# Recurrent jobs of a hybrid trunk step: the inverse's transpose turned by TensorE and copied by ScalarE at each level, in place of a product and an addition

## The chip, the cores and the metric

The kernel runs on one core of one Trainium2 chip. The metric is the device time of one execution in microseconds; the time before is the median of three runs, 2041.28 us (2039.77 to 2044.31).

## The reference, cut to what matters

The program is one inference step of a two-layer trunk over 640 tokens (512 latent, 128 context), all in float32. Layer 0 is attention, layer 1 is a recurrent mixer (a WKV scan and an SSD scan side by side), and each layer ends in a convolutional feed-forward block. The change lies in the WKV scan, which runs once forward and once backward for each of 8 heads of width 64:

```python
def step(S, inp):
    r_t, w_t, a_t, b_t, k_t, v_t = inp
    sa = jnp.einsum('bhvk,bhk->bhv', S, a_t)
    S = S * w_t[:, :, None, :] + sa[..., None] * b_t[:, :, None, :] + v_t[..., None] * k_t[:, :, None, :]
    return S, jnp.einsum('bhvk,bhk->bhv', S, r_t)
```

The kernel does this in chunks of 64 tokens. Within a chunk the coupling of the tokens through `sa` is a triangular 64x64 system, and its inverse is needed for each head, direction and chunk.

## The kernel before, in words

TensorE, VectorE, ScalarE and GpSimd each run a program written out by hand; they meet only at semaphores. The WKV scan is eight jobs (n = 0 to 7): a pair of heads (j = n // 2, one head on partitions 0 to 63, the other on 64 to 127) in one direction (d = n % 2). A job holds ten chunks in two groups g of five. Its tiles are `G_` (the gram products, the first 64 columns of which are the triangular matrix), `X_` (the inverse so far), `XT_` (its transpose), `V_` and the PSUM banks `VX(g)` and `TT(g)`.

The inverse is built in five levels, doubling the block size at each. Per level and group, in the order of `wkv_order`:

- "v": TensorE multiplies `G_` by `X_` into `VX` (ten products of 64x64x64, five chunks by two heads), and VectorE multiplies that by the level's mask into `V_` (line 2587, here "the mask").
- "xt", first half, at levels 1 to 4: TensorE multiplies `XT_` and `V_` into `VX`, and VectorE adds the result to `X_` (line 2593).
- "xt", second half, at all levels: TensorE multiplies `V_` and `XT_` into `TT`, and VectorE adds the result to `XT_` (line 2596).

`wkv_order` is one list of pieces, and all engines walk it in that order. It gives a job 20 slots: for each level "v" of group 0, "v" of group 1, "xt" of group 0, "xt" of group 1. The table `BESIDE` puts pieces of the next job (+1) and of the job before (-1) behind each slot, so that TensorE has other products to do while VectorE masks and adds. Those that matter here are:

- behind slot 3: "scan" of the next job (VectorE line 2538, a scan over 650 elements that waits for GpSimd's line 2657; ScalarE lines 2453 and 2454, two exponentials that wait for the scan);
- behind slots 6 to 8: "prod" of the next job (VectorE lines 2550 to 2569); the last piece also has a copy on ScalarE (line 2460) that waits for the last of these;
- behind slots 7, 9 and 11, when the next job is even: "vt", three turns of values on TensorE, each evacuated by ScalarE (lines 2471 and 2472);
- behind slot 10: "atok" of the next job (TensorE line 2301, which waits for the last "prod"; ScalarE line 2478);
- behind slot 11: "gram" of the next job (TensorE; two of the three banks 4 to 6, which rotate over all side pieces).

Job 0 also carries pieces that run once (`ONCE`), and job 7 has no next job beside it. The names "job n" and "slot" below are these.

Weights of the low-rank factors of the recurrent mixer (`w2s`, `a2s`, `g2s`) are loaded by GpSimd's queue, lines 2955 to 2958, behind five loads of constants and states; TensorE's `first_lora` waits for the semaphore `lora_loaded`, VectorE's `decay_dve` for `ssd_loaded`.

## Time and profile before

| | |
|---|---|
| median of 3 runs | 2041.28 us |
| lowest, highest | 2039.77, 2044.31 us |
| the profiled execution's own time | 2041.86 us |
| its span | 2039.9 us |
| its mean granted TensorE clock | 0.984 |
| TensorE, VectorE, ScalarE, GpSimd busy | 96%, 55%, 34%, 7% of the span |

The profile is of one execution. Its span runs from the first to the last recorded instruction; the execution's own time is 2 us longer. A float32 product appears in the trace as two weight loads (PEld) and two matmuls (PE) when it is an ordinary product, so ten products are 20 records. A matmul's record includes its way through the array, so a row of PE is busier than the array; the weight loads start when the work starts. "Idle before" in the brackets names what ended the wait.

### The profile page before, as it was taken

Reading aid. Unit: us, or ns where it says so; the run is one execution under the profiler, and the core shown is the slowest. Engines: PE = TensorE matmul, PEld = TensorE weight load, DVE = VectorE, ACT = ScalarE, POOL = GpSimd, SP = SyncE. Lnnn points to the kernel's source line nnn. Section 1 sums busy time; section 2 is a strip of 40 time slices with the busy share of each in tenths; the row PEclk is TensorE's granted clock in tenths of the full one; section 3 lists DMA queues with packets and bytes.
Section 4 is the critical chain, followed back from the end, with each engine's and each line's share of the span. In section 5 each row is a group of like instructions: output and inputs, shape, how many; then the busy total and the mean of one; then the engine's idle time right before and its main releaser. Section 6 shows DMA issues by size and latency. Waiting matters only on the chain.

```text
span 2039.9 us, 41373 instructions
## 1 busy us (share of the span) xinstructions
PE 1965.0 (96%) x18397; PEld 1745.2 (86%) x18397; DVE 1115.6 (55%) x2046; ACT 688.9 (34%) x1239; POOL 137.4 (7%) x130
## 2 busy tenths in 40 slices
PE   5999999999999999999999799999999999999997
PEld 3695444899999999999997688888858999999997
DVE  3226754475545562354555877777646555556223
ACT  2322554353323341232346523333204333334111
POOL 2000000000000000000004512222000000000000
PEclk7999999999999999999999899999999999999999
DMA  9123738312222222332220000000211221122322
GB/s 338 49 83 133 271 107 301 109 49 76 83 83 83 68 60 58 85 100 64 62 73 24 7 3 3 3 4 3 91 33 51 83 83 62 63 83 58 86 58 79
DMA packets 141921, 163.92 MB, mean 80 GB/s; under 512 B 2496, under 2 KB 107120, under 8 KB 141744
## 3 DMA queue, kind: packets, MB, share of 16 engines
q1 hardware_dynamic: 138592, 149.96, 22.8%
q0 software_dynamic: 3152, 11.32, 1.5%
q8 instruction: 145, 2.38, 0.5%
q14 instruction: 32, 0.26, 0.0%
HBM read 157.52 MB, written 3.75 MB: 79 GB/s over the span
## 4 chain that ended last, share of the span: by engine, by line
PE 87%; DVE 9%; DMA 1%; issue 1%; ACT 1%; POOL 0%; DVEq 0%; SPq 0%; ACTq 0%; POOLq 0%
PE ps L226 83%; DMA ring<-in_ada_w 1%; DVE g_lo L865 1%; DVE work L2538 1%; PE ps L1253 1%; DVE small L1388 1%; DVE work L498 1%; PE ps L347 1%; ACT work L1317 0%; DVE work L2064 0%; PE ps L462 0%; PE ps L2283 0%; PE ps L2301 0%; DVE work L2596 0%; DVE w_lo L729 0%
## 5 line engine op out<-in xcount | busy, mean ns | idle before, releaser
L226 PE MATMUL ps<-x_hi_r,w_lo 128*128 128x320 f32 (+3 forms) x2240 | 521.8, 308 | 1.6 <-DVE x_lo_r L504 1.3
L226 PE MATMUL ps<-x_hi_r,w_hi 128*128 128x320 f32 (+2 forms) x1792 | 428.8, 311 | 0.9 <-issue 0.9
L226 PE MATMUL ps<-x_lo_r,w_hi 128*128 128x320 f32 (+2 forms) x1792 | 424.9, 308 | 0.0
L226 PEld LDWEIGHTS ps<-x_hi_r,w_lo 128*128 128x128 f32 (+1 forms) x2240 | 373.8, 187 | 3.9 <-DVE x_lo_r L504 1.9
L226 PE MATMUL ps<-work 64*64 64x64 f32 (+6 forms) x4602 | 314.3, 259 | 15.1 <-ACT work L1317 6.7
L226 PEld LDWEIGHTS ps<-x_lo_r,w_hi 128*128 128x128 f32 x1792 | 305.6, 188 | 0.0
L226 PEld LDWEIGHTS ps<-x_hi_r,w_hi 128*128 128x128 f32 x1792 | 303.8, 188 | 1.4 <-issue 1.3
L226 PEld LDWEIGHTS ps<-work 64*64 64x64 f32 (+4 forms) x4602 | 210.7, 145 | 101.1 <-issue 60.0
L678 DVE SCALAR_TENSOR_TENSOR work<-ps,par,work 128x511 f32<-128x511 f32 (+1 forms) x188 | 103.3, 550 | 255.7 <-ACT work L829 245.8
L729 DVE TENSOR_TENSOR w_lo<-ring,w_hi 128x1024 fp32r<-128x1024 f32 (+1 forms) x152 | 158.6, 1079 | 89.3 <-ACT w_hi L718 89.2
L718 ACT ACTIVATE w_hi<-ring 128x1024 fp32r<-128x1024 f32 (+1 forms) x152 | 135.6, 937 | 207.5 <-DMA ring<-in_ffn_down 185.4
L829 ACT ACTIVATE work<-ps,par 128x640 f32<-128x640 f32 x88 | 77.9, 885 | 376.1 <-PE ps L226 376.1
L226 PE MATMUL ps<-g_lo,w_hi 128*128 128x320 f32 (+2 forms) x704 | 174.7, 309 | 0.0
L226 PE MATMUL ps<-work,ring 64*64 64x64 f32 (+3 forms) x2368 | 119.2, 235 | 5.5 <-ACT work L384 2.9
L226 PEld LDWEIGHTS ps<-g_lo,w_hi 128*128 128x128 f32 x704 | 121.4, 188 | 0.0
L226 PEld LDWEIGHTS ps<-work,ring 64*64 64x64 f32 (+2 forms) x2368 | 93.2, 140 | 29.2 <-issue 23.5
L448 DVE SCALAR_TENSOR_TENSOR h<-ps,mods,h 128x512 f32<-128x512 f32 (+2 forms) x76 | 34.9, 495 | 140.0 <-PE ps L226 139.9
L226 PE MATMUL ps<-x_lo_r,w_lo 128*128 128x320 f32 (+2 forms) x416 | 108.2, 310 | 0.0
L680 DVE SCALAR_TENSOR_TENSOR work<-ps,par,work 128x511 f32<-128x511 f32 (+1 forms) x188 | 103.4, 550 | 6.7
L226 PE MATMUL ps<-x_hi_r,w_in_hi 128*128 128x320 f32 (+1 forms) x384 | 89.5, 315 | 0.4 <-issue 0.4
L226 PE MATMUL ps<-x_lo_r,w_in_hi 128*128 128x320 f32 (+1 forms) x384 | 88.0, 310 | 0.0
L226 PE MATMUL ps<-ring,cond 128*32 128x512 f32 x384 | 56.7, 675 | 18.6 <-DMA ring<-in_ada_w 18.6
(378 smaller groups left out, 2452.9 us busy)
## 6 DMA issues: line engine op xcount, KB each, us to landing
ring<-in_ada_w SPq DMA_DIRECT2D x24, 2048.0 KB, 8.0
ring<-in_ffn_up SPq DMA_DIRECT2D x44, 1024.0 KB, 7.0
ring<-in_ffn_down SPq DMA_DIRECT2D x16, 1408.0 KB, 7.0
ring<-in_l_w_in SPq DMA_DIRECT2D x11, 1024.0 KB, 5.2
ring<-in_l_w_out SPq DMA_DIRECT2D x4, 2048.0 KB, 7.9
ring<-in_l_w_in SPq DMA_DIRECT2D x3, 2048.0 KB, 9.0
h<-in_xT POOLq DMA_DIRECT2D x1, 2560.0 KB, 14.7
out_yT<-work POOLq DMA_DIRECT2D x2, 768.0 KB, 4.0
```

The costliest lines, as they stand in the source:

```text
L226: return pe.matmul(out, lhsT, rhs, start=first, stop=last)
L347: ins = pe.matmul(ps_all[:, 1024 * pair + heads * c:1024 * pair + heads * c + heads], squares[:, P * c:P * c + P], col, start=first and c ...
L448: ins = dve.scalar_tensor_tensor(h(m, x, y), psum(u % 2, x, y), gate(m, c), h(m, x, y), ALU.mult, ALU.add)
L498: ins = dve.scalar_tensor_tensor(hn(t, x, y), h(t, x, y), gain(t, c), bank(6 + p)[:, x - a:y - a], ALU.mult, ALU.mult)
L678: ch(dve.scalar_tensor_tensor(acc(a + 1, b), psrc(a, b - 1), w0, acc(a + 1, b), ALU.mult, ALU.add))
L680: ins = dve.scalar_tensor_tensor(acc(a, b - 1), psrc(a + 1, b), w2, acc(a, b - 1), ALU.mult, ALU.add)
L718: act.activation(wh_b[:, SLOT * (f % 2) + w * part:SLOT * (f % 2) + w * part + w], ring[:, SLOT * (n % RING) + w * part:SLOT * (n % RING) ...
L729: dve.tensor_tensor(wl_b[:, at:at + w], ring[:, at:at + w], wh_b[:, SLOT * (f % 2) + w * part:SLOT * (f % 2) + w * part + w].bitcast(F32), ...
L829: act.activation(tile(cacc, 2 * (m % 2) + half), spair(n % 3, cut=up_cut(n)), ACT.Identity, bias=pc(f"ffn_b{l}", half * FT + m), scale=cw( ...
L865: dve.tensor_tensor(gl(t), G(t), gh(t).bitcast(F32), ALU.subtract).then_inc(sg("g_lo"), 1)
L1253: ins = pe.transpose(bank(4)[:, P * kt:P * kt + P] if kt < 4 else bank(5, P), pb[:, P * kt:P * kt + P], ident[:, :])
L1388: dve.tensor_reduce(small[:, c:c + 1], pair_ap(i % 2, 0, w), AXX, ALU.max, negate=True)\
```

## The change

At levels 2 to 5, the transpose is no longer kept up by its own product and addition. TensorE multiplies `X_` (as the stationary operand) by the identity into `TT` at the head of "v", and ScalarE copies `TT` into `XT_` (a new branch of its program at the same place in the list). The "xt" pieces of levels 1 to 4 lose their second product, and VectorE loses its additions of line 2596 there. Level 5 keeps the product and the addition, since the result needed there is the transpose after the last level. The semaphore `wkv_tu` counts two a job instead of ten, and a new one, `wkv_tc`, counts the copies; "xt" of levels 2 to 5 waits for it. Beside that, the three loads of low-rank weights count on `ssd_loaded`, and `first_lora`, `decay_dve` and GpSimd wait for all eight loads.

```diff
@@ TensorE, wkv_pe, kind == "v"
+                    if lev > 1:
+                        for c in range(5 * g, 5 * g + 5):
+                            for e in range(2):
+                                p0, p1 = ROWS[e]
+                                ins = mm(pe, TT(g)[p0:p1, c - 5 * g, :], X_(n)[p0:p1, c, :], ident[p0:p1, p0:p1])
+                        ins.then_inc(sg("wkv_t"), 1)
...
@@ TensorE, wkv_pe, kind == "xt"
-                    if lev > 1 or n > 0:
-                        pe.wait_ge(sg("wkv_tu"), 10 * n + 2 * (lev - 2) + g + 1)
+                    if lev > 1:
+                        pe.wait_ge(sg("wkv_tc"), 8 * n + 2 * (lev - 2) + g + 1)
+                    elif n > 0:
+                        pe.wait_ge(sg("wkv_tu"), 2 * (n - 1) + g + 1)
...
-                    for c in range(5 * g, 5 * g + 5):
-                        for e in range(2):
-                            p0, p1 = ROWS[e]
-                            ins = mm(pe, TT(g)[p0:p1, c - 5 * g, :], V_[p0:p1, c, :], XT_(n)[p0:p1, c, :])
-                    ins.then_inc(sg("wkv_t"), 1)
+                    else:
+                        for c in range(5 * g, 5 * g + 5):
+                            for e in range(2):
+                                p0, p1 = ROWS[e]
+                                ins = mm(pe, TT(g)[p0:p1, c - 5 * g, :], V_[p0:p1, c, :], XT_(n)[p0:p1, c, :])
+                        ins.then_inc(sg("wkv_t"), 1)
@@ ScalarE, wkv_act
+                elif kind == "v" and i[0] > 1:
+                    lev, g = i
+                    act.wait_ge(sg("wkv_t"), 10 * n + 2 * (lev - 2) + g + 1)
+                    act.activation(XT_(n)[:, 5 * g:5 * g + 5, :], TT(g), ACT.Copy).then_inc(sg("wkv_tc"), 1)
@@ VectorE, wkv_dve, kind == "xt"
-                    dve.wait_ge(sg("wkv_t"), 10 * n + 2 * (lev - 1) + g + 1)
-                    x = XT_(n)[:, 5 * g:5 * g + 5, :]
-                    dve.tensor_tensor(x, x, TT(g), ALU.add).then_inc(sg("wkv_tu"), 1)
+                    else:
+                        dve.wait_ge(sg("wkv_t"), 10 * n + 8 + g + 1)
+                        x = XT_(n)[:, 5 * g:5 * g + 5, :]
+                        dve.tensor_tensor(x, x, TT(g), ALU.add).then_inc(sg("wkv_tu"), 1)
@@ VectorE, decay_dve
-            dve.wait_ge(sg("ssd_loaded"), 16 * 5)
+            dve.wait_ge(sg("ssd_loaded"), 16 * 8)
@@ TensorE, first_lora
-                pe.wait_ge(sg("lora_loaded"), 48)
+                pe.wait_ge(sg("ssd_loaded"), 16 * 8)
```

On ScalarE, in job 2 between the exponentials of "scan" and the copies of "atok" (line 2460 is the copy at the end of "prod", line 2478 evacuates "atok"), before:

```order
L2453 ACTIVATE stat<-work 128x650 [waits wkv_scan]
L2454 ACTIVATE work<-work 128x650
L2460 ACTIVATE work<-work 64x10x64 [waits wkv_prod]
L2478 ACTIVATE work<-ps 64x5x64 [waits wkv_atok]
L2478 ACTIVATE work<-ps 64x5x64
```

And of the change, where the same copy of "prod" is line 2469, "atok" is line 2487 and the new copy is line 2495:

```order
L2462 ACTIVATE stat<-work 128x650 [waits wkv_scan]
L2463 ACTIVATE work<-work 128x650
L2495 ACTIVATE work<-ps 128x320 [waits wkv_t] x3
L2469 ACTIVATE work<-work 64x10x64 [waits wkv_prod]
L2495 ACTIVATE work<-ps 128x320 [waits wkv_t]
L2487 ACTIVATE work<-ps 64x5x64 [waits wkv_atok]
```

Three of the new copies (level 2, both groups, and level 3, group 0) stand behind the exponentials, and the fourth (level 3, group 1) behind the copy of "prod".

On TensorE, in job 2 from "prod" to the first "gram" of the next job (`work,ring` are the products of "v", `work 64x64` those of "xt" and of the chain, 128x64 is "atok", `work 128x128 x8` is "gram"), before:

```order
L226 MATMUL ps<-work,ring 64x64 x20
L226 MATMUL ps<-work 64x64 x22
L2301 MATMUL ps<-ident,work 128x64 x10
L226 MATMUL ps<-work 64x64 x20
L226 MATMUL ps<-work 128x128 x8
L226 MATMUL ps<-work 64x64 x2
L226 MATMUL ps<-work,ring 64x64 x10
```

And of the change:

```order
L226 MATMUL ps<-work 64x64 x12
L2301 MATMUL ps<-ident,work 128x64 x10
L226 MATMUL ps<-work 64x64 x10
L226 MATMUL ps<-work 128x128 x8
L226 MATMUL ps<-work 64x64 x2
L226 MATMUL ps<-ident,work 64x64 x10
L226 MATMUL ps<-work,ring 64x64 x10
```

Ten products go from each "xt" piece, and ten with the identity come at the head of each "v" piece of levels 2 to 5: the count over a job stays the same.

## Rows read from the trace of the kernel before

**Rows 1.** The page's first part: busy us, share of the span, instructions.
```profile
PE 1965.0 (96%) x18397; PEld 1745.2 (86%) x18397; DVE 1115.6 (55%) x2046; ACT 688.9 (34%) x1239; POOL 137.4 (7%) x130
```

**Rows 2.** Busy time by window, one window for each job: jobs 0, 2, 3; sum of eight.
```profile
core 0: us, PE busy (x) PEld busy (x) DVE busy (x) ACT busy (x) POOL busy (x), PEclk, DMA share, GB/s
1161.70:1201.00 39.30, 33.68 (x760) 29.73 (x760) 29.66 (x62) 11.83 (x22) 11.29 (x9) 0.91 0.01 3
...
1239.40:1277.00 37.60, 36.15 (x958) 32.89 (x959) 28.57 (x65) 11.74 (x28) 10.60 (x9) 1.00 0.02 4
1277.00:1315.10 38.10, 37.75 (x969) 34.10 (x969) 28.46 (x64) 13.70 (x34) 8.62 (x7) 1.00 0.01 3
...
sum 291.50, PE 280.32 PEld 254.79 DVE 220.03 ACT 90.92 POOL 68.97; mean PE 35.04 PEld 31.85 DVE 27.50 ACT 11.36 POOL 8.62
```

**Rows 3.** By source line: ns min/median/max of the addition and of a ScalarE copy.
```profile
L2596 DVE TENSOR_TENSOR work<-work,ps x80: 475/489/492, 1166.6 to 1453.3; 128x320 f32<-128x320 f32 x80
L2486 ACT ACTIVATE work<-ps x16: 438/438/439, 1160.1 to 1426.9; 128x320 f32<-128x320 f32 x16
```

**Rows 4.** Timeline, job 2: products with the identity (start us, us, what).
```profile
1273.24 0.67 PEld L226 LDWEIGHTS ps<-ident,work 64*64 64x64 f32 x20
```

**Rows 5.** DMA issues (KB each, us to landing) from 896 us; VectorE's first use.
```profile
work<-in_l_g POOLq DMA_DIRECT2D x1, 256.0 KB, 4.3
...
L1795 DVE TENSOR_SCALAR work<-work x1: 485/485/485, 1009.0 to 1009.0; 104x640 f32<-104x640 f32 x1
```

**Rows 6.** Timeline, job 2, from level 1's "xt" to the scan.
```profile
1243.20 2.75 PEld L226 LDWEIGHTS ps<-work 64*64 64x64 f32 x88 [0.44 <-DVE work L2587]
...
1244.00 1.01 POOL L2657 TENSOR_SCALAR work<-work 128x320 f32<-128x320 f32 x1 [2.21 <-ACT work L2447]
...
1246.20 2.78 DVE L2538 TENSOR_TENSOR_SCAN work<-work 128x650 f32<-128x650 f32 x1
```

**Rows 7.** Timeline, job 2, level 3, up to "gram".
```profile
1256.50 0.66 PEld L226 LDWEIGHTS ps<-work,ring 64*64 64x64 f32 x20 [0.36 <-DVE work L2593]
...
1258.03 0.37 PEld L226 LDWEIGHTS ps<-work 64*64 64x64 f32 x10 [0.76 <-DVE work L2587]
...
1259.57 0.16 DVE L2569 COPY work<-stat 128x2 f32<-128x2 f32 x1
...
1259.64 0.48 DVE L2587 TENSOR_TENSOR work<-ps,work 128x320 f32<-128x320 f32 x1
1259.77 0.73 ACT L2460 ACTIVATE work<-work 64x640 f32<-64x640 f32 x1 [9.37 <-DVE work L2569]
1259.78 0.39 PEld L2301 LDWEIGHTS ps<-ident,work 64*128 64x128 f32 x10 [0.51 <-DVE work L2569]
...
1260.24 1.61 PEld L226 LDWEIGHTS ps<-work 64*64 64x64 f32 x44
...
1261.55 0.97 PEld L226 LDWEIGHTS ps<-work 64*128 64x128 f32 x16
```

**Rows 8.** Timeline, job 3, level 3, up to "gram".
```profile
1297.22 0.74 ACT L2460 ACTIVATE work<-work 64x640 f32<-64x640 f32 x1 [2.53 <-DVE work L2565]
...
1297.70 1.24 PEld L226 LDWEIGHTS ps<-work 64*64 64x64 f32 x40
...
1298.65 0.88 ACT L2478 ACTIVATE work<-ps 64x320 f32<-64x320 f32 x2
...
1299.65 0.52 PEld L226 LDWEIGHTS ps<-work 64*128 64x128 f32 x7 [0.33 <-issue]
```

**Rows 9.** Timeline, job 0, levels 2 to 3.
```profile
1170.07 1.38 PE L226 MATMUL ps<-work 64*64 64x64 f32 x40 [1.23 <-DVE work L2587]
...
1170.32 0.73 ACT L2454 ACTIVATE work<-work 128x650 f32<-128x650 f32 x1
...
1176.31 0.80 PE L226 MATMUL ps<-work,ring 64*64 64x64 f32 x20 [1.96 <-DVE work L2593]
...
1179.94 2.40 PE L226 MATMUL ps<-work 64*64 64x64 f32 x40
```

**Rows 10.** Busy time by window in job 0 (columns as in rows 2).
```profile
1172.00:1178.00 6.00, 3.14 (x82) 2.63 (x80) 5.96 (x13) 0.00 (x0) 1.43 (x2) 0.96 0.00 0
1178.00:1184.00 6.00, 5.21 (x71) 4.61 (x73) 5.89 (x15) 1.43 (x3) 0.00 (x0) 0.50 0.02 4
```

More of the change, by code:

```diff
@@ L2357, in wkv_pe @@
                         ins.then_inc(sg("wkv_x"), 1)
-                    for c in range(5 * g, 5 * g + 5):
-                        for e in range(2):
-                            p0, p1 = ROWS[e]
-                            ins = mm(pe, TT(g)[p0:p1, c - 5 * g, :], V_[p0:p1, c, :], XT_(n)[p0:p1, c, :])
-                    ins.then_inc(sg("wkv_t"), 1)
+                    else:
[4 more added lines that the diff above has]
+                        ins.then_inc(sg("wkv_t"), 1)
                 elif kind == "uw":
                     c0, c1 = THIRD[i]
-                    pe.wait_ge(sg("wkv_tu"), 10 * n + (9 if c1 <= 5 else 10))
+                    pe.wait_ge(sg("wkv_tu"), 2 * n + (1 if c1 <= 5 else 2))
                     pe.wait_ge(*evacuated("lkv", n, 1))
@@ L2957, in _ @@
                              (g2s, t_in["l1_g2"])):
-                pool.dma_start(dst, src).then_inc(sg("lora_loaded"), 16)
-            pool.wait_ge(sg("lora_loaded"), 48)
+                pool.dma_start(dst, src).then_inc(sg("ssd_loaded"), 16)
+            pool.wait_ge(sg("ssd_loaded"), 16 * 8)
             first_sum_pool(pool, Chain(pool, "pool_chain"))
```

## The prediction

> **What bounds the kernel now.** I read the page first: TensorE is busy 96% of the span, VectorE 55%, ScalarE 34% [rows 1]. That average says nothing of the stage that changes, so the next view is busy time by window, one window a job [rows 2]. The eight jobs fill 291.5 us, and TensorE is busy for 280.3 of them: 11.2 us are left in which it does nothing. Of those, job 0 has 5.6 (39.30 - 33.68), an even job like job 2 1.45, an odd job like job 3 0.35, and job 7 none. VectorE is busy 28 of 38 us in a job, ScalarE 12 to 14. So TensorE sets the pace, and VectorE makes it wait only in places. The timeline shows where: in job 2 at the second "v" of level 3 (0.36 us for line 2593), at its first "xt" (0.76 us for the mask), at "atok" (0.51 us for the last "prod") [rows 7]. These three make up most of the job's 1.45, and all lie in the stretch from the scan to "atok", in which VectorE has the next job's scan and products in its queue. From "gram" on TensorE hardly waits.
>
> **TensorE's work does not shrink.** Per level and group ten products with the identity replace ten others, 64 sets out and 64 in (8 jobs, 4 levels, 2 groups). Twenty weight loads with the identity take 0.67 us [rows 4], of which the last one's tail is about 0.1, so 0.58 a set. Eighty-eight loads of the "xt" kind take 2.75 us [rows 6]: 0.6 for twenty. Difference: 0. A cheap turn is on view too, ten records for ten turns: "atok", 0.39 us [rows 7]. If the new turns cost that, the sum would fall by 64 x 0.28 = 18 us; the code issues ordinary products, so I take 0. The Trainium skill (TensorEngine Tiling (Array Packing), Restrictions) states that column tiling disables the transpose mode for fp32 input; these outputs fill 64-partition tiles, so by it the -18 us isn't there to be had, and by row and rule alike the sum stays where it is.
>
> **VectorE loses 64 additions** of 0.49 us [rows 3], 0.40 when others follow closely: 26 us. They are worth only what TensorE waited for VectorE, at most the 11.2 us. **ScalarE gains 64 copies**; its copies of this shape take 0.44 us [rows 3], 28 us on an engine that is free two thirds of the stage. But each is now between the turn and "xt", in a queue that is served in order. Two places in the list matter. The level 2 copies stand behind the two exponentials, which wait for the scan; the copy of level 3, group 1 stands behind the copy of "prod" (0.73 us), which waits for the last "prod". I therefore walk three kinds of job.
>
> **Even job (2, 4, 6).** Level 1's "xt" starts at 1243.20 [rows 6]. Without the second products, X of group 1 ends at 1244.4, its addition at about 1245.0, and the scan can start when GpSimd's 1244.00 + 1.01 is done: 1245.1, not 1246.20, so 1.1 earlier. Behind the scan VectorE has two fewer additions before the last "prod", but has to wait a little for TensorE's products; I carry 1.3. The last "prod" (ended 1259.7) ends at 1258.4, and "atok" starts there. Then ScalarE: copy of "prod" 1258.45 to 1259.2, new copy to 1259.65, and only then "xt" of group 1, at 1259.7 (before: 1260.24, after its mask at 1259.64 + 0.48 [rows 7]). Ten products and "gram" follow at about 1260.5, against 1261.55. That is 1.05 earlier, but at this point the old kernel has done six sets for the transpose and the new one four, so 2 x 0.58 = 1.16 are still owed. Net +0.1 a job, three jobs: **+0.3**. What VectorE gave back, the wait for ScalarE takes.
>
> **Odd job (1, 3, 5).** VectorE was hardly late here, so it can give back only the waits at level 2. The copy of "prod" (1297.22 [rows 8]) moves to about 1295.9 and ends at 1296.6; the new copy ends at 1297.05, about when "xt" of group 1 could start. The evacuations of "vt" (0.8) and "atok" (0.88 [rows 8]) stand behind it and end at 1298.7. "Gram" needs the banks of "atok": 1298.75, not the 1298.4 that TensorE would reach. Before: 1299.65. 0.9 earlier less 1.16 owed: +0.26, three jobs: **+0.8**.
>
> **Job 0.** The second exponential ends at 1171.05 and the new copy at 1171.5; "xt" of level 2, at 1170.07 before, waits for it: 1.4 later. VectorE's chain behind it (6 us, which ended in the wait of 1.96 at 1176.31 [rows 9]) starts 0.7 later, saves 0.4 and 0.4 in two additions, and at "gram" I find 0.8 earlier less 1.16 owed: **+0.4**.
>
> **Job 7** has no side work of a next job: a wait for the mask goes (the turn now covers it) and one for the addition to `X_` comes, both some 0.1 to 0.2 us: 0. From level 4 on the copies have a turn, a "v" and side pieces as cover (over 1.5 us for a 0.44 us copy): 0; with less cover each would cost up to 0.44.
>
> **The loads.** They are issued from 897 us, and the last takes 4.3 us to land; VectorE first needs them at 1009.0 [rows 5], TensorE later: 0.
>
> **Sum:** 0.3 + 0.8 + 0.4 + 0 = +1.5 us on the profiled execution's 2041.86, which is 0.6 above the median. On the median: 2041.28 + 1.5 = **2042.8 us**. Its uncertainty is that of a walk, 0.3 to 0.4 a job. A measurement here tells about 0.2%, 4.1 us, from no change.
>
> **Rivals.**
> - *ScalarE's queue decides (slower).* The walks rest on VectorE getting 1.3 us earlier. Each 0.1 us less moves "xt" of group 1, and "gram" with it, 0.1 later in every job with a next one, since the two copies then end the wait. If only the scan's own wait is saved in part (0.6, one set on TensorE), "xt" of group 1 starts at 1259.77 - 0.6 + 0.73 + 0.44 = 1260.35, 0.65 later than in the walk: 7 x 0.7 = 4.9 us on top of 1.5, **2047.7 us**. With nothing gained it would be 7 x 1.3 = 9.1 on top, 2051.9. It decides from 1.3 us downward. For it: both copies surely stand there, and the products that VectorE waits for come from TensorE. Against: the scan waits for two additions of line 2596 ahead of it, which go. Chance 0.13.
> - *VectorE's relief reaches TensorE (faster).* If ScalarE's copies hide, the waits on VectorE go: at most -11.2 [rows 2], 2030; half of that is likelier, as turns and "vt" pieces also wait for other things: **2035.7 us**. Against: the two places in ScalarE's queue. Chance 0.08.
> - *The clock falls (slower).* In job 0 it stands at half from 1178 to 1184, after a stretch in which TensorE was busy 3.14 of 6 us [rows 10]; forty matmuls then take 2.40 us, not 1.38 [rows 9]. If the new turns were to leave the stage at the lower level, each job would be longer by tens of us, over 2200 in all; if only job 0's stretch grows by half, +1.5. Against the first: the identity products of rows 4 ran in a job at clock 1.00 [rows 2]. The Trainium skill (TensorE: Matmul & The Clock Gate, Part 4: PE-mode transpose) says that transpose-mode work doesn't count as busy for the clock; by it a fifth of the inverse's products would cease to count, though these are ordinary products. Chance 0.02 for the large case.
> - *The edit doesn't relieve anything (same).* That is in my walk; it needs no time of its own.
>
> **How the numbers follow.** The forecast has 0.77, with its own range 2038.5 to 2047; it leaves 0.02 below 2037.2 and 0.07 above 2045.4. Faster: 0.07 of the second rival and 0.01 to 0.02 of the forecast's tail: 0.08. Slower: 0.13 + 0.02 + 0.07 = 0.22. Same: 0.70. Range for 8 in 10: 2038.5 to 2048.5, which takes in the queue's rival and leaves out the faster one and the clock.
>
> **What would show it.** Right: 16 rows of line 2596's successor instead of 80, and 64 new ScalarE copies of 0.44 us; TensorE's busy time in the jobs unchanged within 1 us; the scan about 1.1 us earlier in its job; the idle before level 3's "xt" of group 1 ended by ScalarE, some 0.7 us, in the even jobs; job periods within 0.5 us of 37.65 and 38.1. Wrong: "xt" of group 1 released by VectorE and periods under 37.2 (second rival), or periods of 38.3 and more (first), or a clock under 1.00 past job 0. If a set of turns takes over 0.65 us, the term of TensorE's work is wrong, by 64 times the excess.

## The result, and the profile after

| | before | changed |
|---|---|---|
| median of 16 runs each, us | 2040.92 | 2044.93 |
| lowest to highest, us | 2039.24 to 2044.31 | 2038.47 to 2051.42 |
| profiled execution, us (span) | 2041.86 (2039.9) | 2051.21 (2049.4) |
| mean granted clock over the span | 0.984 | 0.984 |

The changed kernel is slower by a ratio of 1.0021, 95% interval 1.0012 to 1.0029: some 4 us, which is right at the 0.2% that a measurement here can tell from no change. The forecast was +1.5 us and a range of 2038.5 to 2048.5 us: the time lies in the range and near the bound between the cases "same" and "slower", but the forecast has less than half of the loss. The mean clock of the span, which has the rest of the program in it, doesn't show the difference. Note also the spread: the standard deviation is 3.0 us over these 16 runs, against 1.7 here and 2.3 to 2.5 in series of 28 to 35 runs of the kernel before. The profiled execution is one of the slowest, so it holds more of the loss than the median does, and I read it beside the profile of a second measurement of the same kernel (e10 below: 2045.38 us). Below, one execution of e9 and one of e12 took several milliseconds; both are left out, and the figures of these two runs rest on eleven.

The first part of the page, busy time by engine, answers to [rows 1]:

```profile
PE 1970.3 (96%) x18397; PEld 1751.2 (85%) x18397; DVE 1084.0 (53%) x1982; ACT 715.0 (35%) x1303; POOL 143.5 (7%) x130
```

TensorE has the same number of instructions, VectorE has 64 fewer, ScalarE 64 more, as foreseen. Busy time by window, one window a job (jobs 0 to 3, 6 and 7, and the sum of eight), answers to [rows 2]:

```profile
core 0: us, PE busy (x) PEld busy (x) DVE busy (x) ACT busy (x) POOL busy (x), PEclk, DMA share, GB/s
1163.80:1206.60 42.80, 35.77 (x760) 31.39 (x762) 26.75 (x55) 14.96 (x30) 11.29 (x9) 0.88 0.01 2
1206.60:1244.70 38.10, 37.36 (x969) 33.91 (x969) 24.82 (x57) 16.98 (x42) 9.89 (x7) 1.00 0.02 3
1244.70:1284.10 39.40, 37.42 (x958) 34.20 (x960) 24.88 (x58) 15.02 (x36) 11.78 (x9) 0.96 0.01 3
1284.10:1322.20 38.10, 37.36 (x969) 33.91 (x969) 24.31 (x56) 16.97 (x42) 9.88 (x7) 1.00 0.01 3
...
1399.80:1437.60 37.80, 35.83 (x960) 32.81 (x962) 24.79 (x57) 15.02 (x36) 11.81 (x9) 1.00 0.01 3
1437.60:1461.20 23.60, 23.51 (x694) 22.59 (x692) 13.65 (x36) 6.26 (x17) 0.00 (x0) 1.00 0.02 5
sum 297.40, PE 282.13 PEld 257.06 DVE 188.38 ACT 117.21 POOL 76.31; mean PE 35.27 PEld 32.13 DVE 23.55 ACT 14.65 POOL 9.54
```

The eight windows take 297.4 us; those of [rows 2] took 291.5, but the last of them ran 1.6 us past job 7's last mask, so the table below, with the same ends for both, is the one to compare: 289.9 and 297.4. The reader is to see three things. VectorE is busy 32 us less over the span (1084.0 against 1115.6) and nothing comes of it. Jobs 1, 3 and 6 are within 0.5 us of the walk. And jobs 0 and 2 (job 4 reads like job 2) stand out, both with a granted clock below 1.00: 0.88 where [rows 2] had 0.91, and 0.96 where they had 1.00.

For a finer table I took each job from its first mask of level 1 to that of the next job; job 7 from its first mask to its last. All from profiled executions, us:

| job | 0 | 1 | 2 | 3 | 4 | 5 | 6 | 7 | sum |
|---|---|---|---|---|---|---|---|---|---|
| before | 39.31 | 38.33 | 37.65 | 38.11 | 37.65 | 38.11 | 37.65 | 23.10 | 289.9 |
| changed | 42.75 | 38.16 | **39.35** | 38.17 | **39.38** | 38.16 | 37.84 | 23.54 | 297.4 |
| changed, e10 | 39.23 | 38.16 | **39.31** | 38.16 | **39.38** | 38.17 | 37.84 | 23.54 | 293.8 |

Jobs 2 and 4 carry a stretch of half clock in both profiles of the changed kernel; job 6, which has the same program, doesn't, and takes 37.84. So an even job has two parts: +0.19 that the program costs, and +1.5 that the clock costs. Job 0 varies most, and of all things it is the one that differs between the two profiles. One caution on reading a whole execution from its profile: the program ahead of job 0 is the same in all kernels here but for the wait for the loads, and yet the first mask of job 0 starts anywhere from 1155.1 to 1165.2 us over the fourteen profiles. Of the 9.5 us between the spans of the two profiles above, 2.1 lie ahead of job 0.

**An even job without a clock fall.** The timeline of job 6, level 3, answers to [rows 7]:

```profile
1418.86 0.16 DVE L2582 COPY work<-stat 128x2 f32<-128x2 f32 x1
...
1418.93 0.48 DVE L2600 TENSOR_TENSOR work<-ps,work 128x320 f32<-128x320 f32 x1
1419.05 0.73 ACT L2469 ACTIVATE work<-work 64x640 f32<-64x640 f32 x1 [3.51 <-DVE work L2582]
1419.07 0.39 PEld L2301 LDWEIGHTS ps<-ident,work 64*128 64x128 f32 x10 [1.09 <-DVE work L2582]
...
1419.81 0.44 ACT L2495 ACTIVATE work<-ps 128x320 f32<-128x320 f32 x1
...
1420.36 2.04 PEld L226 LDWEIGHTS ps<-work 64*64 64x64 f32 x40 [0.91 <-DVE work L2600]
1420.39 2.15 PE L226 MATMUL ps<-work 64*64 64x64 f32 x40 [0.80 <-ACT work L2495]
```

It went as the walk said: the last "prod" ends at 1419.02, ScalarE copies it, then makes the new copy until 1420.25, and only then does TensorE go on with "xt" of group 1, 0.80 us of idle that its own row puts down to line 2495. (The weight loads' row names VectorE's mask, which had ended at 1419.41; the copy came last.) What the walk had too kindly: "prod" comes 1.13 us earlier in its job (1419.02 - 1399.78 against 1259.73 - 1239.36), not 1.3, and "xt" 0.30 earlier, not 0.54. Ahead of "atok" TensorE idles 1.09 us where it idled 0.51 [rows 7], since it has 0.58 us less to do before it.

**An odd job.** Timeline of job 3, which answers to [rows 8]:

```profile
1303.58 0.44 ACT L2495 ACTIVATE work<-ps 128x320 f32<-128x320 f32 x1
...
1304.16 0.80 PE L226 MATMUL ps<-work 64*64 64x64 f32 x20 [0.44 <-ACT work L2495]
...
1304.71 0.88 ACT L2487 ACTIVATE work<-ps 64x320 f32<-64x320 f32 x2
...
1305.70 1.32 PEld L226 LDWEIGHTS ps<-work 64*128 64x128 f32 x20 [0.51 <-issue]
```

"Gram" starts 21.63 us into the job (1305.70 - 1284.07) where it started at 22.64 (1299.65 - 1277.01): 1.01 earlier, against 0.9 in the walk, less the 1.16 still owed. The job is 0.06 longer.

**Job 0.** Timeline at level 2, which answers to [rows 9]:

```profile
1171.62 0.47 DVE L2600 TENSOR_TENSOR work<-ps,work 128x320 f32<-128x320 f32 x1
...
1172.39 0.73 ACT L2463 ACTIVATE work<-work 128x650 f32<-128x650 f32 x1
...
1173.03 0.74 ACT L2495 ACTIVATE work<-ps 128x320 f32<-128x320 f32 x2
...
1173.59 1.33 PE L226 MATMUL ps<-work 64*64 64x64 f32 x20 [2.46 <-ACT work L2495]
```

Here too the wait is the one foreseen: the mask ends at 1172.09, the copy behind the second exponential at about 1173.5, and "xt" goes 1.5 us later than the mask would let it. Behind it the clock comes in. Job 0 of e10, by window (columns as above):

```profile
1161.50:1200.70 39.20, 32.87 (x760) 28.89 (x762) 26.65 (x55) 14.96 (x30) 11.30 (x9) 0.96 0.01 3
```

The same 760 matmuls keep TensorE busy for 32.87 us there, for 35.77 in the first profile of the change and for 33.68 before; it is idle for 6.3, 7.0 and 5.6 us. So in job 0 the waits cost 0.7 to 1.4 us, and the rest of the difference goes with the granted clock (0.96, 0.88 and 0.91).

**The clock in job 2.** Busy time in windows around the two idles of level 3 (columns as above):

```profile
1258.60:1262.00 3.40, 3.18 (x104) 3.03 (x102) 3.40 (x8) 0.44 (x1) 1.54 (x2) 1.00 0.00 0
1262.00:1265.40 3.40, 1.65 (x43) 1.31 (x40) 2.93 (x9) 1.39 (x3) 0.37 (x1) 1.00 0.03 7
1265.50:1268.80 3.30, 3.30 (x42) 2.96 (x41) 0.67 (x2) 0.43 (x1) 0.00 (x0) 0.50 0.00 0
1268.90:1272.20 3.30, 3.30 (x92) 3.11 (x90) 2.60 (x6) 0.61 (x2) 0.00 (x0) 1.00 0.02 5
```

The idle before "atok" and the one before "xt", 1.1 and 0.9 us, now stand close together: TensorE is busy 1.65 of 3.4 us. Right after it the granted clock is 0.50 (1.2 GHz) for 3.4 us, TensorE gets 42 matmuls done where the next window has 92, and then it is 1.00 (2.4 GHz) again. The kernel before had no low clock in jobs 1 to 7.

### The profile page after: what moved, and what is told of

It reads as the page before. It is cut to its first block, busy times and chain, and to the rows that moved or that the text cites. A ratio compares the mean times of both kernels' runs of the same rounds, so it can differ in the third digit from the quotient of the medians.

```text
span 2049.4 us, 41373 instructions
## 1 busy us (share of the span) xinstructions
PE 1970.3 (96%) x18397; PEld 1751.2 (85%) x18397; DVE 1084.0 (53%) x1982; ACT 715.0 (35%) x1303; POOL 143.5 (7%) x130
## 4 chain that ended last, share of the span: by engine, by line
PE 87%; DVE 8%; ACT 2%; DMA 1%; issue 1%; POOL 0%; DVEq 0%; SPq 0%; POOLq 0%; ACTq 0%
PE ps L226 84%; DMA ring<-in_ada_w 1%; DVE g_lo L865 1%; PE ps L1253 1%; DVE small L1388 1%; DVE work L498 1%; PE ps L347 1%; ACT work L1317 0%; DVE work L2064 0%; PE ps L462 0%; PE ps L2283 0%; DVE w_lo L729 0%; DVE work L2571 0%; DVE x_lo_r L504 0%; DVE work L2573 0%
## 5 line engine op out<-in xcount | busy, mean ns | idle before, releaser
L226 PE MATMUL ps<-work 64*64 64x64 f32 (+8 forms) x3322 | 281.5, 279 | 19.8 <-ACT work L1317 7.6
L226 PEld LDWEIGHTS ps<-work 64*64 64x64 f32 (+5 forms) x3322 | 176.9, 152 | 105.9 <-issue 62.5
L226 PE MATMUL ps<-work,ring 64*64 64x64 f32 (+3 forms) x2368 | 124.5, 235 | 2.9 <-ACT work L384 2.9
```

What stands on the lines that cost most here:

```text
L226: return pe.matmul(out, lhsT, rhs, start=first, stop=last)
```

## The experiments

My theory after the result: an instruction in ScalarE's queue takes back what VectorE gave, and the idle thus bunched brings the clock down. The rivals were that the products with the identity cost more than those they replace, that the loads do, and that a lighter VectorE is worth nothing to TensorE anyway. Times beside each other are from one chip.

| run | median us (runs) | before beside it | ratio, 95% interval |
|---|---|---|---|
| e1_copy_first | 2040.65 (12) | 2040.25 | 1.0004 [0.9995, 1.0013] |
| e2_no_copy | 2039.07 (11) | 2040.25 | 0.9996 [0.9986, 1.0005] |
| e3_turn_twice | 2043.69 (12) | 2040.25 | 1.0018 [1.0008, 1.0029] |
| e4_vector_copies | 2044.46 (11) | 2040.25 | 1.0024 [1.0014, 1.0034] |
| e5_both_ahead | 2037.77 (12) | 2040.33 | 0.9992 [0.9980, 1.0003] |
| e6_masks_ahead | 2046.98 (6) | 2040.33 | 1.0032 [1.0020, 1.0044] |
| e7_before_masks_ahead | 2041.38 (12) | 2040.33 | 1.0007 [0.9998, 1.0017] |
| e8_loads_only | 2040.39 (11) | 2040.33 | 1.0000 [0.9992, 1.0009] |
| e9_gap_filled | 2043.34 (11) | 2040.69 | 1.0016 [1.0007, 1.0025] |
| e10_change_again | 2046.26 (12) | 2040.69 | 1.0030 [1.0018, 1.0043] |
| e11_job0_filled | 2037.01 (12) | 2040.69 | 0.9983 [0.9973, 0.9993] |
| e12_before_filled | 2039.95 (11) | 2039.94 | 1.0004 [0.9995, 1.0012] |

And the job periods of their profiles, us, measured as above:

| run | 0 | 1 | 2 | 3 | 4 | 5 | 6 | 7 |
|---|---|---|---|---|---|---|---|---|
| e1 | 42.74 | 37.70 | 37.11 | 37.70 | 37.11 | 37.70 | 37.11 | 23.54 |
| e2 | 40.56 | 37.70 | 37.11 | 37.70 | 37.11 | 37.70 | 37.11 | 23.54 |
| e3 | 41.22 | 38.17 | 37.84 | 38.16 | 37.84 | 38.16 | 37.84 | 24.12 |
| e4 | 41.71 | 38.10 | 37.59 | 38.09 | 37.58 | 38.10 | 37.59 | 23.54 |
| e5 | 41.99 | 37.71 | 37.11 | 37.69 | 37.10 | 37.69 | 37.10 | 23.54 |
| e6 | 41.41 | 39.02 | 37.69 | 40.51 | 37.69 | 39.02 | 39.17 | 23.54 |
| e7 | 39.83 | 38.91 | 37.82 | 38.70 | 37.75 | 38.69 | 37.74 | 23.10 |
| e8 | 39.40 | 38.32 | 37.66 | 38.10 | 37.65 | 38.11 | 37.65 | 23.10 |
| e9 | 43.22 | 38.16 | 37.83 | 38.16 | 37.83 | 38.16 | 37.83 | 24.12 |
| e11 | 40.96 | 37.69 | 37.10 | 37.70 | 37.10 | 37.70 | 37.10 | 23.54 |
| e12 | 38.49 | 38.31 | 37.65 | 38.10 | 37.65 | 38.10 | 37.65 | 23.10 |

Periods of one kernel repeat to 0.02 us where the clock is whole, so they tell far smaller differences apart than the medians do; job 0 doesn't repeat.

### e1: one pair exchanged in ScalarE's queue

```diff
+        def act_order():
+            order = list(wkv_order())
+            def ahead(piece, of):
+                if piece in order and of in order and order.index(piece) > order.index(of):
+                    order.remove(piece)
+                    order.insert(order.index(of), piece)
+            for m in range(JOBS):
+                ahead(("v", m, (3, 1)), ("prod", m + 1, 4))
+            return order
...
-            for kind, n, i in wkv_order():
+            for kind, n, i in act_order():
```

> The change, with one pair of ScalarE instructions exchanged in each job: the copy of the turned transpose of level 3, group 1 stands ahead of the copy that ends prod of the next job, not behind it. Nothing else moves. Theory A (queue): that order makes xt of level 3, group 1 wait about 0.9 us for ScalarE in each of seven jobs, and the idle time that it bunches together is what lets TensorE's clock fall in some jobs. Then the wait is ended by VectorE's mask, the undisturbed even job is 0.8 us shorter (37.84 to about 37.0), fewer stretches at half clock, and the kernel comes to about 2039 us, 0.1% under the kernel before. Theory B (the turns themselves cost more than the products they replace): no change from 2044.9. Theory C (the clock falls whatever ScalarE does): 1 to 2 us less at most, half-clock stretches as often as in the change.

The new copy of level 3, group 1 now stands ahead of the copy of "prod". Timeline of e1's job 2, level 3 (the mask is line 2611 here):

```profile
1259.21 0.48 DVE L2611 TENSOR_TENSOR work<-ps,work 128x320 f32<-128x320 f32 x1
1259.33 0.73 ACT L2480 ACTIVATE work<-work 64x640 f32<-64x640 f32 x1 [1.90 <-DVE work L2593]
1259.35 0.39 PEld L2301 LDWEIGHTS ps<-ident,work 64*128 64x128 f32 x10 [1.09 <-DVE work L2593]
...
1259.81 0.66 PEld L226 LDWEIGHTS ps<-work 64*64 64x64 f32 x20
```

"Xt" follows the mask by 0.12 us; the second idle is gone. The periods fall by 0.73 in an even and 0.46 in an odd job, to 37.11 and 37.70, which is 0.54 and 0.41 under the kernel before: that is what the relief of VectorE is worth once ScalarE doesn't take it back. No low clock shows in jobs 1 to 7. By window, jobs 0 to 2:

```profile
1159.60:1202.40 42.80, 37.09 (x760) 32.43 (x762) 26.75 (x55) 14.95 (x30) 11.30 (x9) 0.84 0.01 2
1202.40:1240.10 37.70, 37.38 (x969) 33.94 (x971) 24.84 (x58) 16.96 (x42) 9.87 (x7) 1.00 0.01 3
1240.10:1277.20 37.10, 35.86 (x958) 32.79 (x960) 24.80 (x58) 15.11 (x36) 11.78 (x9) 1.00 0.02 4
```

The time is that of the kernel before, not below it. The six jobs give back 0.63 + 3 x 0.54 + 2 x 0.41 = 3.1 us and job 7 costs 0.44; in this profile job 0 takes it, 42.74 us with the clock at 0.84. Its copies still stand behind the exponentials, but waiting isn't what makes it longer: TensorE is idle for 5.7 us in it (5.6 before) and busy for 37.09 (33.68 before) with as many matmuls. Theory A had the even jobs right (0.8 foreseen, 0.73 measured) and the median 1.6 us too low.

### e2: no copies and no waits for them

```diff
-                    if lev > 1:
-                        pe.wait_ge(sg("wkv_tc"), 8 * n + 2 * (lev - 2) + g + 1)
-                    elif n > 0:
+                    if lev == 1 and n > 0:
...
-                elif kind == "v" and i[0] > 1:
-                    lev, g = i
-                    act.wait_ge(sg("wkv_t"), 10 * n + 2 * (lev - 2) + g + 1)
-                    act.activation(XT_(n)[:, 5 * g:5 * g + 5, :], TT(g), ACT.Copy).then_inc(sg("wkv_tc"), 1)
```

> The change without ScalarE's 64 copies and without TensorE's waits for them: the transpose is turned into PSUM and not used, so levels 2 to 5 work with the transpose of level 1. What the copies cost in all. Theory A (queue): as with the pair exchanged, and job 0 gets back its wait behind the exponentials (1.4 us) too: about 2037.5 us. Theory B (turns cost more): within 1 us of the change, 2044. Theory C (clock): within 2 us of the change.

It leaves out the transposes of levels 2 to 5: the turns are computed and never copied. Its periods are those of e1 to 0.01 us. So in jobs 1 to 7 the one exchanged pair is all that ScalarE cost, and the other seven copies of a job are free there, as the prediction had them from level 4 on, and at level 2 and level 3, group 0 as well. Job 7 takes 23.54 here too, 0.44 over before, with no copy in it: that loss isn't ScalarE's. Where it arises the timeline of the changed kernel shows, at level 1 and at level 4 of job 7:

```profile
1439.96 0.49 DVE L2600 TENSOR_TENSOR work<-ps,work 128x320 f32<-128x320 f32 x1 [1.85 <-PE ps L226]
...
1440.51 1.00 PEld L226 LDWEIGHTS ps<-work 64*64 64x64 f32 x28
...
1457.40 0.27 DVE L2643 SCALAR_TENSOR_TENSOR work<-ps,work 128x64 f32<-128x64 f32 x1
...
1457.72 0.91 PEld L226 LDWEIGHTS ps<-work 64*64 64x64 f32 x28 [0.22 <-DVE work L2643]
```

At level 1, "xt" of group 1 waits for its mask, which ends at 1440.45 (some 0.2 us); at level 4 a product of the "chain" of the job before waits 0.22 us for an addition of VectorE's. The profile of the kernel before shows no such idle at either place, where ten more products, the second half of "xt", stood ahead.

### e3: the turn of level 3, group 1 twice

```diff
-                        for c in range(5 * g, 5 * g + 5):
+                        for c in list(range(5 * g, 5 * g + 5)) * (2 if i == (3, 1) else 1):
```

> The change, with the ten turns of level 3, group 1 done twice in each job (0.58 us of TensorE, the same result). They stand ahead of the stretch in which TensorE waits for prod and then for ScalarE (2.2 us in an even job). Theory A (queue): the wait swallows them in jobs 0, 2, 4, 6 and in part in the odd jobs: 0 to +2 us over the change, and with TensorE less idle there not more half-clock stretches, perhaps fewer. Theory B (TensorE bound throughout, turns are what costs): 8 x 0.58 = +4.6 us, 2049.5.

TensorE does a set of 0.58 us more ahead of the wait, in every job. By window, jobs 1 and 2 (columns as above):

```profile
1196.30:1234.50 38.20, 37.97 (x989) 34.55 (x990) 24.90 (x57) 17.02 (x42) 9.87 (x7) 1.00 0.01 3
1234.50:1272.30 37.80, 36.24 (x978) 33.26 (x978) 24.80 (x57) 15.00 (x36) 11.77 (x9) 1.00 0.02 4
```

Ten more products a job (20 records), and the periods, 38.17 and 37.84, are those of the undisturbed jobs of the change. In job 7, which has no such wait, they cost 0.58 (24.12 - 23.54), as the set was priced. So TensorE's work ahead of the wait doesn't set the end, and an identity set costs what the walk took. Theory B's 2049.5 us is ruled out; the medians of e3 and of the change can't be told apart. Note also the clock: with the idle ahead of "atok" shortened to 0.68 us, none of jobs 1 to 7 holds a low clock in this profile. And yet the median is 3.4 us above the kernel before.

### e4: VectorE makes the copies

```diff
+                    if lev > 1:
+                        dve.wait_ge(sg("wkv_t"), 10 * n + 2 * (lev - 2) + g + 1)
+                        dve.tensor_copy(XT_(n)[:, 5 * g:5 * g + 5, :], TT(g)).then_inc(sg("wkv_tc"), 1)
                     dve.wait_ge(sg("wkv_v"), 10 * n + 2 * (lev - 1) + g + 1)
```

ScalarE loses its four lines for the copy, as in e2.

> The change, with the 64 copies of the turned transpose on VectorE, each ahead of the mask of the same piece, not on ScalarE. What VectorE's relief was worth. Walk: each copy takes VectorE 0.4 us, as the additions that went did; between the scan and the last prod there are three of them and a fourth ahead of the mask of level 3, group 1. If the relief of VectorE was worth 1.2 us a job (theory A), the kernel is 6 to 9 us slower than the change, about 2052. If VectorE's relief is worth nothing and the wait for ScalarE is what counts (its opposite), it is faster than the change, 2040.

A miss of both figures. VectorE gets its load back, by window in jobs 1 and 2:

```profile
1200.90:1239.00 38.10, 37.50 (x969) 33.94 (x971) 27.69 (x66) 13.58 (x34) 9.87 (x7) 1.00 0.01 3
1239.00:1276.50 37.50, 35.82 (x958) 32.68 (x958) 27.75 (x65) 11.74 (x28) 11.77 (x9) 1.00 0.01 4
```

The periods of jobs 2 to 6 are within 0.1 us of the kernel before (job 1: 0.23 less), so without the relief of VectorE the new form of the transpose is worth next to nothing, and costs nothing, in these jobs. The median is as slow as the change's, though, and jobs 0 (41.71, with 10.2 us of half clock in it) and 7 are where its profile shows the loss. Over its 11 executions the mean granted clock is 0.9845, against 0.9872 over the 35 of the kernel before beside them: its loss goes with a lower clock too.

### e5: the copies of level 2 ahead as well

```diff
                 ahead(("v", m, (3, 1)), ("prod", m + 1, 4))
+                ahead(("v", m, (2, 0)), ("scan", m + 1, 0))
+                if m == 0:
+                    ahead(("v", m, (2, 1)), ("scan", m + 1, 0))
```

> The change with the pair exchanged as in e1, and besides the new copy of level 2, group 0 ahead of the two exponentials of scan in every job (in job 0 that of group 1 too). Theory A (queue): only job 0 was held up by the exponentials (xt of level 2 at 1173.56 against a mask done at 1172.09). Its wait of 1.5 us goes, with it a part of the idle time after which the clock falls there; jobs 1 to 7 keep the periods of e1 (37.1, 37.7). Job 0 from about 42.7 to 40 or less, kernel about 2038.5 us, 0.1% under the kernel before. Theory C (job 0 is long because VectorE's side pieces keep TensorE idle and the clock at half whatever ScalarE does): as e1, 2040.6.

The periods of jobs 1 to 6 stay at e1's (e2 had said so). Job 0 doesn't come to 40 us or less, as theory A had it: it takes 41.99, still has 13.7 us of half clock, and TensorE is idle in it for 5.2 us. So the place of the copies of level 2 isn't what makes job 0 long; theory C was nearer there. The median is 2.6 us below the kernel before, e2's was 1.2 below; both intervals hold 1, so neither is settled as faster.

### e6 and e7: the last products of "prod" and the mask in another order

Both edit the table that places the side work; e6 on top of e5, e7 on the kernel before, with no other edit:

```diff
-            (("prod", 1, 3), ("prod", 1, 4)), (("chain", -1, 2), ("vt", 1, 1)), (("atok", 1, 0),),
-            (("vt", 1, 2), ("gram", 1, 0), ("chain", -1, 3)), (("gram", 1, 1),), (("chain", -1, 4),),
+            (), (("chain", -1, 2), ("prod", 1, 3), ("prod", 1, 4), ("vt", 1, 1)), (),
+            (("atok", 1, 0), ("vt", 1, 2), ("gram", 1, 0), ("chain", -1, 3)), (("gram", 1, 1),), (("chain", -1, 4),),
```

> e5, and the last two pieces of prod stand behind the second v of level 3 (so that VectorE does its mask first), and atok behind the second xt of level 3, not between the two. TensorE then waits once for prod where it waited for prod and for the mask. Walk of an even job: xt of group 1 can start when that of group 0 ends, atok when prod ends, gram 1.1 us earlier than in e1: even job 37.1 to 36.0, odd job, which waits 0.3 us there, 37.7 to 37.3, kernel 3 to 5 us under e5, about 2034.5. If VectorE is the bound in that stretch, prod gets later by the mask and half of that is lost: 2036.5.

> The kernel before, without the change, with only the two moves of e6 (prod behind the second v, atok behind the second xt of level 3). What the order of the list gives by itself. With the old additions VectorE's queue in that stretch is longer by 1.2 us, and TensorE has ten more products in each xt to fill the wait for prod: even job from 37.65 to about 36.9, odd job 38.11 to 37.9, kernel about 2038 us. If the gain of e6 comes from the relief of VectorE alone, nothing: 2040.5.

A failure, 2046.98 us where 2034.5 was foreseen (e7: 2041.38, foreseen 2038): the move takes the wait from the mask and puts another in its place. Timeline of e6, job 3:

```profile
1295.63 0.73 ACT L2483 ACTIVATE work<-work 64x640 f32<-64x640 f32 x1 [2.41 <-DVE work L2592]
1295.65 0.39 PEld L2301 LDWEIGHTS ps<-ident,work 64*128 64x128 f32 x10 [0.46 <-DVE work L2592]
...
1296.39 0.38 ACT L2494 ACTIVATE work<-ps 64x256 f32<-64x256 f32 x1
...
1297.21 0.31 PEld L2290 LDWEIGHTS ps<-ident,work 128*128 128x128 f32 x3 [1.17 <-ACT work L2495]
```

The copy of "prod" and the evacuations of "vt" are now due at one moment, and TensorE waits 1.17 us for ScalarE. Jobs 1, 3, 5 and 6 are longer by over a microsecond, and jobs 3 and 6 hold a stretch of half clock again. On the kernel before the same move costs 0.1 to 0.6 a job. The order as it stood was the better one for both.

### e8: the loads alone

The kernel before with the change's edits to the loads' semaphores and their waits (the last two hunks of the diff above, and GpSimd's issue and wait):

```diff
-                pool.dma_start(dst, src).then_inc(sg("lora_loaded"), 16)
-            pool.wait_ge(sg("lora_loaded"), 48)
+                pool.dma_start(dst, src).then_inc(sg("ssd_loaded"), 16)
+            pool.wait_ge(sg("ssd_loaded"), 16 * 8)
```

> The kernel before, with only the change's third part: the three loads of low-rank weights count on ssd_loaded, and first_lora, decay_dve and GpSimd wait for all eight loads. They land by about 906 us and are first needed at 1009: all theories, no change, ratio within 0.1% of 1.

Nothing, 1.0000. This part is closed.

### e9 and e10: the idle filled, and the change beside it

```diff
-                        for c in range(5 * g, 5 * g + 5):
+                        for c in list(range(5 * g, 5 * g + 5)) * ((3 - n % 2) if i == (3, 1) else 1):
```

> The change, with the ten turns of level 3, group 1 done three times in even jobs and twice in odd jobs (12 sets more, 7 us of TensorE, the same result), all ahead of the stretch in which TensorE waits for prod and then for ScalarE. Theory A2 (the wait for ScalarE costs 0.2 us a job by itself, and the rest of the loss is that TensorE, idle for 2.2 us of 3.5 there, now and then gets half its clock for 3.4 us): the periods stay 37.84 and 38.16 where the clock is full, no half-clock stretch falls in jobs 1 to 7, the scatter shrinks, and the kernel is 1.5 to 2.5 us faster than the change measured beside it although it does more. Theory D (half-clock stretches cost nothing in the median): as e3, the same as the change or 1 us more.

> The change once more, on the same chip as e9 and e11. All theories: 2044.9 and ratio 1.002, with half-clock stretches of 3.4 us in some of the even jobs, the even jobs without one at 37.84, with one at about 39.4.

This is the test of the clock: the same kernel with more work for TensorE and nothing else changed, run beside the change itself. By window, job 2 of e9, then job 2 of e10 and a stretch in it (columns as above):

```profile
1246.60:1284.40 37.80, 36.79 (x998) 33.85 (x1000) 24.75 (x58) 15.02 (x36) 11.79 (x9) 1.00 0.01 4
```

```profile
1238.90:1278.20 39.30, 37.33 (x958) 34.11 (x960) 24.80 (x58) 15.02 (x36) 11.81 (x9) 0.96 0.02 4
...
1259.40:1262.80 3.40, 3.34 (x38) 3.03 (x39) 0.49 (x1) 0.67 (x2) 0.00 (x0) 0.50 0.00 0
```

With 20 more products (40 records) than the change has, job 2 takes 37.83 us instead of 39.31, as does job 4; no low clock is left in e9's jobs 1 to 7. That shows, in the profiles, that the 1.5 us of these jobs are the clock's. That the clock fell there because TensorE idled is what the counts say: a fall in four of six even jobs in the two profiles of the change, in none of three in e9 and in none of three in e3, which differ from it only in products ahead of "atok". It rests on one profile each. In the time it shows less surely: 2043.34 against 2046.26, with intervals that overlap. Each execution also lists its mean granted clock. Over 12 of e10 the mean is 0.9842 (0.981 to 0.987), over 11 of e9 0.9870 (0.982 to 0.990), over the 28 of before beside them 0.9878. Among e10's own runs the longer ones tend to be those with the lower clock: 2040.06 us at 0.987, 2048.37 at 0.982. So the spread of e10 goes in large part with its clock. But e9 is still 2.7 us slower than the kernel before, with the clock nearly as high: the falls in jobs 2 and 4 are not all of the loss.

### e11 and e12: job 0 filled too, and the same on the kernel before

e11 is e5 with turns repeated in job 0 (level 2, group 1 four times, level 3 three times each) and level 3, group 1 twice in even jobs. e12 is the kernel before with products of "v" repeated in job 0 at the same places.

```diff
@@ e11, on top of e5
-                        for c in range(5 * g, 5 * g + 5):
+                        for c in list(range(5 * g, 5 * g + 5)) * ({(2, 1): 4, (3, 0): 3, (3, 1): 3}.get(i, 1) if n == 0 else 2 if i == (3, 1) and n % 2 == 0 else 1):
@@ e12, on the kernel before, products of "v"
-                    for c in range(5 * g, 5 * g + 5):
+                    for c in list(range(5 * g, 5 * g + 5)) * ({(2, 1): 3, (3, 0): 4, (3, 1): 3}.get(i, 1) if n == 0 else 1):
```

> e5 (both copies ahead) with turns repeated where TensorE waits: in job 0 those of level 2, group 1 four times, of level 3, group 0 and group 1 three times, in jobs 2, 4, 6 those of level 3, group 1 twice (10 sets more, 5.8 us of TensorE, the same result). Theory A2: job 0 no longer runs at half clock for 7 to 14 us (42.0 us in e5's profile), it comes to 39 or less, the other jobs keep 37.1 and 37.7: 2035, 0.25% under the kernel before. Theory D: as e5 or slower, 2038 to 2041.

> The kernel before, with only job 0's v pieces repeated where TensorE then waits: level 2, group 1 three times, level 3, group 0 four times, level 3, group 1 three times (7 sets more, 4 us of TensorE, the same result). A control for e11: how much of its gain is the filling of job 0 and how much the change with its copies ahead. Theory A2: the repeats lie in waits of 1.4, 2.1 and 1.6 us and cost nothing, the half-clock stretch of job 0 (6.8 us in the profile of before) shortens or goes: 0 to 1.5 us faster, ratio 0.9995, so that most of e11's 0.17% is the change. Rival: filling by itself brings e11's gain, ratio 0.9983.

By window, jobs 0 and 2 of e11:

```profile
1157.60:1198.50 40.90, 38.06 (x900) 34.15 (x901) 26.62 (x54) 15.07 (x30) 11.31 (x9) 0.91 0.01 3
...
1236.20:1273.30 37.10, 36.27 (x978) 33.29 (x980) 24.79 (x58) 15.14 (x36) 11.80 (x9) 1.00 0.02 4
```

e11 is the fastest kernel of the study: 2037.01 us, ratio 0.9983 [0.9973, 0.9993], with nothing left out. It beats the kernel before by 3.7 us in the medians and the change by 9.2 beside it. The filling by itself is not the reason: e12 took job 0 down to 38.49, without a low clock, and its time is still 1.0004 (0.9995 foreseen). Job 0 of e11 didn't do what was foreseen, 39 us or less: it takes 40.96, with 6.8 us of half clock in it. What of e11's gain over e5 is the filling stays unsettled, their intervals overlap; its mean clock, 0.9879 over 12 runs against 0.9858 for e5's, speaks for some of it.

## Why the prediction was right and wrong

- **TensorE's work: +0.** Right. Counts are equal, and e3 prices one more set at 0.58 us in job 7, the prediction's own figure. No run shows the products with the identity failing to count as work for the clock: jobs 1 to 7 of e1 stand at 1.00 with all of them in. (They are 8 of the 28 sets of an inverse, not a fifth as the prediction says.) The Trainium skill (TensorE: Matmul & The Clock Gate, Part 4: PE-mode transpose) says otherwise of transpose-mode work only, and the new turns are ordinary products. The ten turns of "atok" are issued as transposes, and they are the only work between the two idles of level 3; no run separates what they count for, so that rival of the idles alone stays open.
- **Even job: +0.1 each, measured +0.19.** Right in mechanism, shown by e1: the scan starts 1.15 us earlier in job 2, as foreseen (1.1), and what VectorE gives back (0.54) is taken by the wait for ScalarE (0.73). "I carry 1.3" should have been 1.13.
- **Odd job: +0.26 each, measured +0.05** in jobs 3 and 5 and -0.17 in job 1. Right in mechanism, a little too dear. The relief is 0.41 to 0.6, the wait 0.46.
- **Job 7: 0, measured +0.44.** The step that a wait for the mask goes and one for the addition to `X_` comes failed in its second half: TensorE shows no wait for the addition there. Instead two idles of some 0.2 us each come where the second product of "xt" no longer stands ahead of a wait, one for the mask of level 1, one in the chain of the job before (shown at e2). With no side work of a next job nothing else covers them.
- **The loads: 0.** Right (e8).
- **The sum of the program's part.** 3 x 0.19 - 0.17 + 2 x 0.05 + 0.44 = +0.9 us without job 0: the forecast's +1.5, with job 0's +0.4 in it, has the size of it.
- **The clock: the step that failed.** The rival was written as "if the new turns were to leave the stage at the lower level", with "if only job 0's stretch grows by half, +1.5" beside it, and was given 0.02 and no place in the sum. The prediction had named "a clock under 1.00 past job 0" as a sign that it was wrong, and that came. I had worked out every idle of level 3 and did not ask how they lie to each other. Before, 0.36, 0.76 and 0.51 lay at three places over 3.6 us (1.63 in all, by the weight loads' rows; the 1.45 that they were set against is counted on the matmuls' rows); now 1.09 and 0.91 lie within 2.4 us, and both profiles of the change show a stretch of 3.4 us at half speed behind them in jobs 2 and 4, 1.5 us each, +3.0 in all. In the median it may be less: e9 and e3, whose profiles hold no such stretch, are still 2.7 and 3.4 us above the kernel before. That the time still lies in the range owes something to luck: its upper end was drawn for another cause, a longer wait for ScalarE, and it also took in a loss that the sum did not have.
- **Job 0: +0.4, too small.** The wait was placed rightly (1.5 us, foreseen 1.4), but its price is not one number: 39.2 and 42.8 in two profiles of one kernel. What the average run pays I can only bound: take the difference of the medians, less what the profile's jobs 1 to 7 explain. What is left for job 0, and for all that lies ahead of it, is 0.0 in the change and 1.6 in e10, 3.0 in e1, 1.4 in e2, 1.9 in e3, 4.2 in e4, 1.2 in e9, but 0.1 in e5 and -1.0 in e11, where the copies of level 2 stand ahead of the exponentials. For e1: 2040.65 - 2040.25 is +0.4, jobs 1 to 7 are 247.97 - 250.60 = -2.6, and 3.0 is left. Each such figure is uncertain by 1.5 to 2 us; together they say some 2 us, of which I had 0.4.
- **The books.** +0.9 (program, jobs 1 to 7), +3.0 (clock, jobs 2 and 4), 0 to 2 (job 0): 3.9 to 5.9, against medians of +4.0 and +5.6 in the two measurements of the change. They close no better than the 1.5 to 2 us of a median's uncertainty, so they don't check the clock's share.
- **The rival "VectorE's relief reaches TensorE"** did not happen in the change, and e1, e2 and e5 show how far it reaches when ScalarE is out of the way: 3.1 us over six jobs, not the 5.6 that it was priced at. **"ScalarE's queue decides"** was the right mechanism for the even jobs and no larger than in the walk.

Still open: why job 0 takes from 39.2 to 43.2 us in the profiles of the changed kernels, with 3.4 to 13.7 us of half clock in it, where the kernel before and e8 have 39.3 and 39.4 with 6.8. ScalarE's queue isn't all of it, since e2 has no copies, e4 has them on VectorE and e5 has them ahead, and all three leave a long job 0 in the profile; the low stretches vary between executions, and each kernel has one or two profiles. Open too is why job 6, with the same idles as jobs 2 and 4, kept its clock in both profiles.

## What to carry to other kernels

When work moves to an idle engine, its utilisation says little: look at what the instruction stands behind in that engine's queue. Here one copy behind one that waited for a busy engine took back all that 32 us less work on VectorE were worth, and exchanging the two brings the time from 1.0021 or 1.0030 of the old one to 1.0004. And after summing the idle of TensorE, list where it lies: idles that move together may cost more in clock than each costs by itself. Filling such a gap with repeated work is a cheap test of whether the clock is the cause; it wants more than one profile a side where, as here, the falls don't come in every job.

## What the runs showed of the hardware

- Two idles of 1.1 and 0.9 us within 2.4 us, in a job in which TensorE is busy 95% of the time, were followed by 3.4 us at half the clock (1.2 GHz), which cost 1.5 us, in jobs 2 and 4 of two profiles. With the first filled (e9), the first cut to 0.68 us (e3) or the second removed (e1) the clock held in the one profile of each. The same idles in job 6 had no such consequence.
- Products added ahead of a wait were free: nine sets in e9's jobs 1 to 6, 5.2 us of TensorE's time, left each period where an undisturbed job of the change has it, within 0.02 us.
- With the clock whole, a job's period repeats to 0.02 us between kernels and chips, while medians of 12 runs are known to 0.1%: where a stage is periodic, its period is the finer measure.
